# Two alternating sets of semaphores, a projection slab loaded a block earlier, and store waits moved

## The chip, the cores and the metric

The kernel runs on one core of one Trainium2 chip. The metric is the device time of one execution in microseconds; the median of three runs is 5510.2 us (5507.91 to 5512.08).

## What is computed

Two layers of a hybrid trunk, for a prompt of 512 tokens and 8 samples of 8 new tokens (576 rows of 1024, float32). Cut to what matters:

```python
h = _rmsnorm(x, norm_mix[l])
qkv_a, z_a, a_a, b_a, qkv_b, u_c, gate_logits = _split_cols(h @ w_in[l])
o_a, conv_new, delta_new = _deltanet(qkv_a, z_a, a_a, b_a, conv0, delta0, ...)   # gated delta rule, chunks of 128
o_b, wins_new = _dilated_branch(qkv_b, pos0, prompt, wins0)                      # windowed attention, 3 groups of 4 heads
o_c, pool_new = _pool_branch(u_c, pool0, pos0, w_pool[l], pool_scale[l])
gates = sigmoid(gate_logits).reshape(B, T, 3, 1024)
merged = gates[:, :, 0] * (o_a @ wb_a) + gates[:, :, 1] * (o_b @ wb_b) + gates[:, :, 2] * (o_c @ wb_c)
x = x + merged @ w_out[l]
x = x + _peer(_rmsnorm(x, norm_ffn[l]), ...)   # 128 experts per row, fetched by index, up and down
```

The states of the delta rule, the last rows of keys and values of each window group, and the last rows of the two other branches are outputs too.

## The kernel before, in words

TensorE (PE), VectorE (DVE), ScalarE (ACT), GpSimd (POOL) and SyncE (SP) each get a stream of instructions written out by hand, with waits on semaphores. The work of a layer is nine stages, each one `nc.Block()`, and a block ends only when all five engines have arrived: each engine ends with a DRAIN, tells POOL, and POOL releases them all. SP issues most DMAs, POOL issues the gathers, the gate weights and the gate rows, ACT some small ones.

1. `norm_stage` (L287 on): RMS norm of x and its transposed copy hT.
2. `delta_in` (L442): the first 2048 columns of the projection, convolution, norms.
3. `delta_chunks`, first block (L640): per chunk decays and a triangular inverse. POOL starts by copying old cache rows from input to output in HBM.
4. `delta_chunks`, second block (L874): SP loads the delta states of the samples (four loads of 512 KB, L878), PE runs the recurrence over the chunks and then the samples' states; SP stores them (L880, L883) and waits for all five stores.
5. `window_in` (L1288): 2304 columns of the projection in six slabs of 384 columns (1.5 MB each), double buffered. SP issues them through `load_slabs` (L392), the first two at once, later ones when PE has freed the place. PE multiplies (L1321), ACT copies out (L1351), DVE and POOL rotate queries and keys, SP stores key rows (L1280, L1283), PE transposes (L1336), ACT copies (L1358) and then issues twelve stores of value rows. SP waits for the key stores; the value stores are waited for by POOL in the next stage. POOL also loads the first three gate weights.
6. `window_prompt` (L1400): attention of the prompt in 16 units of a row tile and a head. Between the scores PE computes the merge gates (L1220), two halves per unit; ACT copies them out (L1231), POOL stores each finished one to HBM and loads the next weights (L1207, L1202). SP loads the first caches for the next stage.
7. `window_samples` (L1570): attention of the samples over their caches and the rest of the 24 gates. SP loads the pool stage's first slab. POOL waits at the end until all gate stores have landed (L1576).
8. `pool_stage` (L1864): projection to 1536 columns, sliding means, maps. POOL first clears the margins of `ext`; SP loads the first weights and gates for the merge.
9. `score_expert_stage` (L2373): the merge and w_out, the second norm, the routing, then 576 gathers of 128 rows of 8 KB (L2404), a dot product each on DVE (L2429), a diagonal on ACT (L2501) and two products on PE (L2587).

After the last layer `norm_stage` runs once more, and a block stores the result.

Semaphores only count up. There is one set, which all stages share, and a few that are kept (`keep`) and waited for with values that grow by layer. After each stage `clear_semaphores` (L273) adds a block of its own, in which POOL clears the set in two ranges (L282) while the others wait. There are 20 such blocks: nine per layer, one after the initial loads, one in the last norm.

The order in SBUF around the change (in floats per partition): AT_MIX 0 holds hT and branch outputs, AT_LATE 8192 the delta block's zT and cc, later the merge slots, AT_WORK 16384 the work of each stage.

Of the kernel before, what the change touches and what calls it, by code (L numbers as in the profile page):

```python
# [124 lines left out]
class Semaphores:  # L125
# [3 lines left out]
    def __init__(self, make, keep):  # L129
# [4 lines left out]
        self.map1 = make("map1")  # L134
# [6 lines left out]
        self.link_pool = make("link_pool")  # L141
# [16 lines left out]
        self.pool_b = make("pool_b")  # L158
        self.pool_c = make("pool_c")
        self.pool_d = make("pool_d")  # L160
        self.filled = make("filled")
        self.copied = make("copied")
        self.numbers = make("numbers")
        self.paced = make("paced")
        self.dots_done = make("dots_done")
        self.downs_done = make("downs_done")
        self.gelus = make("gelus")
        self.weighted = make("weighted")
        self.diagonal = make("diagonal")
        self.summed = make("summed")  # L170
        self.x_copied = make("x_copied")
        self.gate_in = make("gate_in")
        self.gate_exp = make("gate_exp")
        self.gate_ready = make("gate_ready")
        self.routed = make("routed")
        self.scored = make("scored")
        self.doubled = make("doubled")
        self.values_stored = keep("values_stored")
        self.gcum = make("gcum")
        self.masked = make("masked")  # L180
        self.started = make("started")
        self.inv_sum = make("inv_sum")
        self.inv_done = make("inv_done")
        self.u_sum = make("u_sum")
        self.u_copied = make("u_copied")
        self.x_sum = make("x_sum")
        self.squared = make("squared")
        self.w_out_in = make("w_out_in")
        self.branch_sum = make("branch_sum")
        self.branch_read = make("branch_read")  # L190
        self.gate_open = make("gate_open")
        self.merged_done = make("merged_done")
        self.out_sum = make("out_sum")
        self.x_added = make("x_added")
        self.hT_a = make("hT_a")
        self.hT_b = make("hT_b")
        self.scored0 = make("scored0")
# [5 lines left out]
        self.st_scaled = make("st_scaled")  # L203
        self.ab_read = make("ab_read")
        self.banks_read = make("banks_read")
        self.stored2 = keep("stored2")
        self.pool_slab = keep("pool_slab")
        self.merge_in = [keep(f"merge_in{i}") for i in range(MERGE_RING)]
# [77 lines left out]
def norm_stage(nc, g, gamma, rows, sb, transposed=True, sources=()):  # L286
# [61 lines left out]
    clear_semaphores(nc, g)  # L348
# [64 lines left out]
def delta_stage(nc, g, t, o, l):  # L413
# [12 lines left out]
    clear_semaphores(nc, g)  # L426
    delta_chunks(nc, g, t, o, l, zT, cc, vecs, ab, heads, gb, chunks)
# [5 lines left out]
def delta_in(nc, g, t, o, l, w_in, zT, cc, vecs, ab, heads, ring, slabs, sb):  # L433
# [8 lines left out]
    with nc.Block() as block:  # L442
# [157 lines left out]
SQ = 4 * 512 + H * NS  # L600


def delta_chunks(nc, g, t, o, l, zT, cc, vecs, ab, heads, gb, sb):
# [36 lines left out]
    with nc.Block() as block:  # L640
# [181 lines left out]
        def _(pool):  # L822
            heads2 = lambda ap: ap.rearrange("b t v h d -> b t v (h d)")
# [31 lines left out]
    clear_semaphores(nc, g)  # L855
# [18 lines left out]
    with nc.Block() as block:  # L874
        @block.sync
        def _(sp):
            for h in range(H):
                sp.dma_start(st[:, h], layer(t["state_delta"], l)[:, h].rearrange("b d e -> d b e")).then_inc(s.loaded, 16)  # L878
            sp.wait_ge(s.dve_b, 4)
            sp.dma_start(layer(o["delta_p"], l)[0].rearrange("h d e -> d h e"), state[:, 0]).then_inc(s.stored, 16)  # L880
            for h in range(H):
                sp.wait_ge(s.dve_c, 2 * h + 2)
                sp.dma_start(sd_out[:, h].rearrange("b d e -> d b e"), st[:, h]).then_inc(s.stored, 16)  # L883
            sp.wait_ge(s.stored, 16 * 5)
# [138 lines left out]
        def _(pool):  # L1023
            def spread(half):
# [155 lines left out]
    clear_semaphores(nc, g)  # L1180
# [53 lines left out]
AT_CACHES = AT_WORK + 7296  # L1234
# [3 lines left out]
def window_stage(nc, g, t, o, l, slots):  # L1238
    w_in = layer(t["w_in"], l)
    late, sb = g.space(AT_LATE), g.space(AT_WORK)  # L1240
    qkT = late("qkT", [P, 12, SEQ])
    vals_s, qkT_s = late("vals_s", [P, SW]), late("qkT_s", [P, 12, NS])
    gates = Gates(nc, g, t, l, sb)
    low = sb.above()
    vals = sb("vals", [P, 4, SW])
    window_in(nc, g, t, o, l, w_in, vals, vals_s, qkT, qkT_s, gates, sb.above())
    clear_semaphores(nc, g)
    places = g.space(AT_CACHES)
    caches = Caches(g, t, l, places)
    window_prompt(nc, g, l, vals, qkT, gates, caches, g.space(AT_PROMPT))  # L1250
    clear_semaphores(nc, g)
    window_samples(nc, g, t, l, vals_s, qkT_s, gates, caches, low, places, g.space(AT_LATE + SLOT), slots)
    clear_semaphores(nc, g)
# [6 lines left out]
def window_in(nc, g, t, o, l, w_in, vals, vals_s, qkT, qkT_s, gates, sb):  # L1260

    s = g.s
    ring = sb("ring", [P, 2, KT * WB])
# [5 lines left out]
    heads2 = lambda ap: ap.rearrange("b t v h d -> b t v (h d)")  # L1269
# [3 lines left out]
    def store_rows(eng, kv, done):  # L1273

        count = 0
        for i in range(3):
            src = lambda n: (qk[0:ROWS[n], n, SW + i * 256:SW + (i + 1) * 256], value(n)[:, i * 256:(i + 1) * 256])[kv]
            for n in range(3 if i == 0 else 0, 4):
                at = n * P if i else 0
                eng.dma_start(heads2(layer(o[f"win{i}_p"], l))[0, at:at + P, kv], src(n)).then_inc(done, 16)  # L1280
                count += 16
            keep = min(GROUPS[i][0], PAST + NT)
            eng.dma_start(heads2(layer(o[f"win{i}_s"], l))[:, keep - NT:keep, kv], src(4)).then_inc(done, 16)  # L1283
            count += 16
        assert count == VALUE_STORES
        return count

    with nc.Block() as block:  # L1288
        @block.sync
        def _(sp):  # L1290
            load_slabs(sp, g, ring, [rows_of(w_in)[:, :, C_B + i * WB:C_B + (i + 1) * WB] for i in range(6)])
            sp.wait_ge(s.dve_a, 2 * TILES)
            sp.wait_ge(s.stored, store_rows(sp, 0, s.stored))
# [3 lines left out]

# [46 lines left out]
        def _(act):  # L1344
            for i in range(6):
                for n in range(TILES):
# [32 lines left out]
def window_prompt(nc, g, l, vals, qkT, gates, caches, sb):  # L1379
# [20 lines left out]
    with nc.Block() as block:  # L1400
        @block.sync
        def _(sp):
            caches.ahead(sp)
# [1297 lines left out]
```

## Time and profile before

| | us |
|---|---|
| median of three runs | 5510.2 |
| profiled execution | 5511.6 |
| its span, first to last instruction | 5509.8 |
| PE busy | 4729.3 (86%) |
| DVE busy | 3007.9 (55%) |
| POOL busy | 1542.9 (28%) |
| ACT busy | 1240.7 (23%) |
| DMA over the span | 260 GB/s, 1432.12 MB |

The profile is of one execution. Busy time counts neither waits nor branches nor the issue of DMAs by SP and ACT. The mean granted clock of TensorE is 0.96 of full speed.

### The profile page before, as it was taken

Reading aid. Unit: us, or ns where it says so; the run is one execution under the profiler, and the core shown is the slowest. Engines: PE = TensorE matmul, PEld = TensorE weight load, DVE = VectorE, ACT = ScalarE, POOL = GpSimd, SP = SyncE. Lnnn points to the kernel's source line nnn. Section 1 sums busy time; section 2 is a strip of 40 time slices with the busy share of each in tenths; the row PEclk is TensorE's granted clock in tenths of the full one; section 3 lists DMA queues with packets and bytes.
Section 4 is the critical chain, followed back from the end, with each engine's and each line's share of the span. In section 5 each row is a group of like instructions: output and inputs, shape, how many; then the busy total and the mean of one; then the engine's idle time right before and its main releaser. Section 6 shows DMA issues by size and latency. Waiting matters only on the chain. (4 is left out here: it accounts for less than half of the span.)

```text
span 5509.8 us, 50367 instructions
## 1 busy us (share of the span) xinstructions
PE 4729.3 (86%) x17274; PEld 2768.6 (50%) x17274; DVE 3007.9 (55%) x7296; ACT 1240.7 (23%) x3097; POOL 1542.9 (28%) x1418
## 2 busy tenths in 40 slices
PE   7889999999998777777788899999998987777776
PEld 5765777755444322332167667777554443223321
DVE  4532222226767789975455223231267777999654
ACT  2211220102222233321112112101122222333211
POOL 0321100003444444444304121000044444444442
PEclk9999999999999999999999899999999999999999
DMA  2222232318999999999812232324099999999997
GB/s 100 77 68 85 80 113 79 125 35 342 414 407 411 422 421 421 421 419 421 347 64 77 72 107 66 107 77 143 24 393 416 403 414 421 421 421 421 418 421 303
DMA packets 338777, 1432.12 MB, mean 260 GB/s; under 512 B 27548, under 2 KB 156438, under 8 KB 190602
## 3 DMA queue, kind: packets, MB, share of 16 engines
q0 software_dynamic: 177376, 1268.07, 56.5%
q1 hardware_dynamic: 155214, 157.65, 9.0%
q10 hardware_dynamic: 5932, 3.19, 0.2%
q8 instruction: 137, 2.24, 0.2%
q14 instruction: 118, 0.97, 0.0%
HBM read 1400.18 MB, written 49.44 MB: 263 GB/s over the span
## 5 line engine op out<-in xcount | busy, mean ns | idle before, releaser
L2587 PE MATMUL ps<-early,diag 128*128 128x512 f32 (+1 forms) x3584 | 1693.8, 620 | 390.1 <-ACT diag L2501 389.7
L2404 POOL DMA_INDIRECT early<-in_peer,ids x896 | 979.7, 1093 | 1816.1 <-PE ps L2587 1241.1
L2587 PEld LDWEIGHTS ps<-early,diag 128*128 128x128 f32 (+1 forms) x3584 | 659.4, 191 | 1382.3 <-issue 722.2
L2429 DVE SCALAR_TENSOR_TENSOR early<-early,rows 128x1024 f32<-128x1024 f32 x896 | 1084.5, 1223 | 455.2 <-DMA early<-in_peer,ids 453.8
L2587 PE MATMUL ps<-late,diag 128*128 128x512 f32 (+1 forms) x1024 | 491.0, 626 | 147.3 <-ACT diag L2501 147.1
L2501 ACT ACTIVATE diag<-consts_sb,weight 128x128 f32<-128x128 f32 (+1 forms) x1152 | 392.9, 388 | 702.6 <-DVE weight L2439 697.6
L2587 PEld LDWEIGHTS ps<-late,diag 128*128 128x128 f32 (+1 forms) x1024 | 182.8, 187 | 454.0 <-ACT diag L2501 244.4
L2493 ACT ACTIVATE gel<-dot 128x2 f32<-128x2 f32 x576 | 117.3, 204 | 1292.8 <-DVE early L2429 979.8
L1220 PE MATMUL ps<-hT,gate_ring 128*128 128x288 f32 x1536 | 404.6, 419 | 1.2 <-ACT gate_out L1231 1.2
L2404 POOL DMA_INDIRECT late<-in_peer,ids x256 | 280.3, 1095 | 355.3 <-PE ps L2587 324.0
L2429 DVE SCALAR_TENSOR_TENSOR late<-late,rows 128x1024 f32<-128x1024 f32 x256 | 309.4, 1223 | 121.6 <-DMA late<-in_peer,ids 121.4
L1220 PEld LDWEIGHTS ps<-hT,gate_ring 128*128 128x128 f32 x1536 | 291.6, 194 | 97.8 <-issue 22.2
L1321 PE MATMUL ps<-ring,hT 128*128 128x384 f32 x768 | 255.5, 493 | 26.5 <-DMA ring<-in_w_in 23.3
L2523 PE MATMUL ps<-late 128*128 128x288 f32 x1024 | 259.3, 408 | 5.4 <-ACT late L2174 5.4
L2523 PEld LDWEIGHTS ps<-late 128*128 128x128 f32 x1024 | 195.1, 191 | 78.3 <-issue 23.3
L1492 DVE TENSOR_TENSOR sc<-ps,consts_sb 128x256 f32<-128x256 f32 (+3 forms) x96 | 43.9, 458 | 347.0 <-PE ps L1444 248.4
L1207 POOL DMA_DIRECT2D gate_rows<-gate_out x48 | 27.3, 569 | 698.5 <-ACT gate_out L1231 698.5
L1321 PEld LDWEIGHTS ps<-ring,hT 128*128 128x128 f32 x768 | 146.4, 193 | 131.8 <-DMA ring<-in_w_in 26.4
L362 PE MATMUL ps<-hT,ring 128*128 128x288 f32 x512 | 169.8, 414 | 4.5 <-PEq L278 3.9
L363 PE MATMUL ps<-hT,ring 128*128 128x288 f32 x512 | 167.9, 410 | 0.0
L2439 DVE TENSOR_TENSOR weight<-gel,gates 128x2 f32<-128x2 f32 x576 | 93.1, 162 | 130.7 <-ACT gel L2493 124.7
L1950 PE MATMUL ps<-hT,slot 128*128 128x288 f32 x384 | 127.9, 415 | 11.0 <-PEq L278 11.0
(364 smaller groups left out, 5526.1 us busy)
## 6 DMA issues: line engine op xcount, KB each, us to landing
gate_ring<-in_w_in POOLq DMA_DIRECT2D x48, 512.0 KB, 4.7
ring<-in_w_in SPq DMA_DIRECT2D x12, 1536.0 KB, 6.4
slot<-in_w_branch SPq DMA_DIRECT2D x16, 1152.0 KB, 6.5
ring<-in_w_in SPq DMA_DIRECT2D x8, 2048.0 KB, 9.4
late<-in_peer_query SPq DMA_DIRECT2D x32, 512.0 KB, 17.3
early<-in_peer,ids POOLq DMA_INDIRECT x896, 19.4
gate_rows<-gate_out POOLq DMA_DIRECT2D x48, 288.0 KB, 2.4
slot<-gate_rows SPq DMA_DIRECT2D x16, 864.0 KB, 8.4
```

The costliest lines, as they stand in the source:

```text
L362: nc.tensor.matmul(part_a(g, u), weights(k), rhs(k)[:, 0:HALF], start=k == 0, stop=k == nk - 1)
L363: last = nc.tensor.matmul(part_b(g, u), weights(k), rhs(k)[:, HALF:TOK], start=k == 0, stop=k == nk - 1)
L1220: last = nc.tensor.matmul(g.ps[:, bank, 0:HALF], self.ring[:, i % GATE_RING, k, :], g.hT[:, k, at:at + HALF], start=k == 0, stop=k == KT - 1)
L1321: last = nc.tensor.matmul(g.ps[0:P, u % 4, 0:WB], g.hT[:, k, cols(n)], w[:, k, :], start=k == 0, stop=k == KT - 1)
L1950: nc.tensor.matmul(bank_a(p), weights, g.hT[:, k, 0:HALF], start=k == 0, stop=k == KT - 1)
L2404: pool.indirect_dma_start(place(q), None, table_rows, bass.IndirectOffsetOnAxis(ap=ids[:, n, c:c + 1], axis=0)).then_inc(s.pair[PLACE[q]], 16)
L2429: nc.vector.scalar_tensor_tensor(out=up, in0=up, scalar=1.0, in1=rows[:, n, :], op0=ALU.mult, op1=ALU.mult, accum_out=dot[:, i % 2, k:k + ...
L2439: nc.vector.tensor_tensor(weight[:, i % 2], gel[:, i % 2], gates[:, n, c0:c0 + GROUP], ALU.mult).then_inc(s.weighted, 1)
L2493: nc.scalar.activation(gel[:, i % 2], dot[:, i % 2], ACT.Gelu).then_inc(s.gelus, 1)
L2501: nc.scalar.activation(diag[:, q % DIAGS, 0:ROWS[n]], table(g, "ident" if ROWS[n] == P else "ident2"), ACT.Copy, scale=weight[:, i % 2, k: ...
L2523: last = nc.tensor.matmul(g.ps[:, 4 + i % 2, 0:HALF], late.ring[:, u % Q_RING, k, :], late.hT[:, k, a * HALF:(a + 1) * HALF], start=k == 0 ...
L2587: ins = nc.tensor.matmul(g.ps[0:r, 2 * (n % 2) + m, :], diag[:, q % DIAGS, 0:r], place(q)[:, D + m * 512:D + (m + 1) * 512], start=False, ...
```

## The change

- A stage takes the other of two sets of semaphores than the stage before it (`next_semaphores`), and POOL clears the set that isn't in use at the start of the block. Semaphores that only the expert stage or only the stages of the delta and window branches use are made once and cleared in a stage where nobody uses them. The 20 clearing blocks are gone.
- The first slab of the window projection gets a place of its own (over keys and values of the delta block that are dead by then) and is loaded in the second delta block, behind the states. `window_in` loads slabs 1 to 5.
- SP no longer waits for the stores of the delta states in that block. ACT, DVE and POOL wait for them in `window_in`, ahead of their first write to the places that are stored.
- SP no longer waits for the key stores in `window_in`, but in `window_prompt`, ahead of the cache loads.
- The value stores are issued by SP at the start of `window_prompt`, no longer by ACT at the end of `window_in`.
- POOL no longer waits for the gate stores at the end of `window_samples`; it does at the start of `pool_stage`, before its memsets, and SP does before it loads the first gates. ACT now waits for the memsets before its first copy, DVE before its first.
- Tiles move to make this possible: values to AT_LATE, transposed queries and keys to AT_WORK, scores of the samples in two places, slots in the other order.

```diff
-def clear_semaphores(nc, g):
-    with nc.Block() as block:
-        @block.gpsimd
-        def _(pool):
-            for first, last in g.runs:
-                pool.sem_clear(range(first, last + 1))
+def next_semaphores(g):
+    g.turn = 1 - g.turn
+    g.s = g.sets[g.turn]
+
+def clear_other_set(pool, g):
+    for first, last in g.runs[1 - g.turn]:
+        pool.sem_clear(range(first, last + 1))
+
+def clear_single(pool, runs):
+    for first, last in runs:
+        pool.sem_clear(range(first, last + 1))
...
# norm_stage; every other block with clear_other_set alone at the start of POOL's stream
+            @block.gpsimd
+            def _(pool):
+                clear_other_set(pool, g)
+                clear_single(pool, g.experts_runs)
...
-    clear_semaphores(nc, g)
+    next_semaphores(g)
...
# delta_chunks, second block
             for h in range(H):
                 sp.dma_start(st[:, h], layer(t["state_delta"], l)[:, h].rearrange("b d e -> d b e")).then_inc(s.loaded, 16)
+            sp.dma_start(slab[:], window_slab(t, l, 0)).then_inc(s.win_slab, 16)
             sp.wait_ge(s.dve_b, 4)
-            sp.dma_start(..., state[:, 0]).then_inc(s.stored, 16)
+            sp.dma_start(..., state[:, 0]).then_inc(s.delta_stored, 16)
             for h in range(H):
                 sp.wait_ge(s.dve_c, 2 * h + 2)
-                sp.dma_start(..., st[:, h]).then_inc(s.stored, 16)
-            sp.wait_ge(s.stored, 16 * 5)
+                sp.dma_start(..., st[:, h]).then_inc(s.delta_stored, 16)
...
-AT_CACHES = AT_WORK + 7296
+AT_VALUES, AT_SLAB = AT_LATE + 1536, AT_LATE + 4608
+AT_CACHES = AT_WORK + 10368
...
# window_in
+    ring = (slab, sb("ring", [P, KT, WB]))
...
-            load_slabs(sp, g, ring, [rows_of(w_in)[:, :, C_B + i * WB:C_B + (i + 1) * WB] for i in range(6)])
+            for i in range(1, 6):
+                if i >= 2:
+                    sp.wait_ge(s.slab_free, i - 1)
+                sp.dma_start(ring[i % 2][:], window_slab(t, l, i)).then_inc((s.slab0, s.slab1)[i % 2], 16)
             sp.wait_ge(s.dve_a, 2 * TILES)
-            sp.wait_ge(s.stored, store_rows(sp, 0, s.stored))
+            store_rows(sp, o, l, 0, lambda n, i: qk[...], s.keys_stored)
...
         def _(pool):
+            clear_other_set(pool, g)
+            pool.wait_ge(s.delta_stored, DELTA_STORES * (l + 1))
...
         def _(pe):
-                slab_ready(pe, g, i)
-                w = slab_view(ring, i, KT, WB)
+                w = ring[i % 2]
+                if i == 0:
+                    pe.wait_ge(s.win_slab, 16 * (l + 1))
+                else:
+                    pe.wait_ge((s.slab0, s.slab1)[i % 2], 16 * ((i + 1) // 2))
...
         def _(act):
+                    if i == 5 and n == 0:
+                        act.wait_ge(s.delta_stored, DELTA_STORES * (l + 1))
...
-            act.wait_ge(s.act_b, 6 * TILES)
-            store_rows(act, 1, s.values_stored)
...
         def _(dve):
+            dve.wait_ge(s.delta_stored, DELTA_STORES * (l + 1))
...
# window_prompt
         def _(sp):
+            store_rows(sp, o, l, 1, lambda n, i: (vals[:, n] if n < 4 else vals_s[0:NS])[...], s.values_stored)
+            sp.wait_ge(s.keys_stored, (l + 1) * VALUE_STORES)
             caches.ahead(sp)
...
         def _(pool):
+            clear_other_set(pool, g)
+            clear_single(pool, g.mixing_runs)
...
# window_samples
             for i in range(first_gate // 2, GATE_UNITS):
                 gates.store(pool, i)
-            for i in range(GATE_OUT):
-                pool.wait_ge(s.gate_stored[i], 16 * (l + 1) * (GATE_UNITS // GATE_OUT))
...
# pool_stage
         def _(sp):
             sp.wait_ge(s.slab_free, 2)
+            for i in range(GATE_OUT):
+                sp.wait_ge(s.gate_stored[i], 16 * (l + 1) * (GATE_UNITS // GATE_OUT))
             merge.load(sp, 0)
...
         def _(pool):
+            clear_other_set(pool, g)
+            for i in range(GATE_OUT):
+                pool.wait_ge(s.gate_stored[i], 16 * (l + 1) * (GATE_UNITS // GATE_OUT))
             for i in range(2):
                 nc.gpsimd.memset(ext[:, i, :, 0:PBUF], 0.0).then_inc(s.filled, 1)
...
         def _(act):
+            act.wait_ge(s.filled, 2)
...
         def _(dve):
-                dve.wait_ge(s.filled, 2)
...
+            dve.wait_ge(s.filled, 2)
```

## Rows read from the trace of the kernel before

**Rows 1.** Windows by stage: bounds, length, busy PE, PEld, DVE, ACT, POOL, clock, DMA, GB/s.

```profile
374.56:540.43 165.87, 149.88 (x636) 92.64 (x636) 32.01 (x20) 22.28 (x51) 26.61 (x13) 0.95 0.26 83
...
1021.81:2752.00 1730.19, 1452.10 (x3774) 683.93 (x3774) 1150.61 (x3015) 422.61 (x1140) 619.97 (x576) 0.97 0.89 363
...
3756.90:5486.84 1729.94, 1451.99 (x3774) 683.64 (x3774) 1151.38 (x3015) 422.69 (x1140) 640.05 (x576) 0.97 0.89 363
```

**Rows 2.** Waits of SP's queue over the span: us in total, times, longest.

```profile
SPq L278 <- PEq L278: 13.9, 20, 0.7
...
SPq L874 <- DMA out_delta_s<-st: 5.6, 2, 2.8
```

**Rows 3.** DRAINs of lines 278, 1400 and 1570: ns min/median/max, first and last start.

```profile
L278 POOLq DRAIN  x20: 34/41/47, 17.1 to 5501.4; - x20
...
L1400 POOLq DRAIN  x2: 4948/4980/5012, 744.5 to 3478.5; - x2
...
L1570 SPq DRAIN  x2: 122/122/122, 776.5 to 3511.7; - x2
...
L1570 POOLq DRAIN  x2: 1109/1112/1114, 876.4 to 3610.3; - x2
```

**Rows 4.** Timeline of the pool stage's start, ACT's first copy: start us, us.

```profile
888.98 0.40 ACT L1980 COPY ext<-ps 128x288 f32<-128x288 f32 x1 [15.48 <-PE ps L1951]
```

**Rows 5.** The page's DMA issues: KB each, median us to landing.

```profile
gate_ring<-in_w_in POOLq DMA_DIRECT2D x48, 512.0 KB, 4.7
...
gate_rows<-gate_out POOLq DMA_DIRECT2D x48, 288.0 KB, 2.4
```

**Rows 6.** Timeline from the delta block's end into the window projection, layer 0.

```profile
367.34 3.35 SPq L883 DMA_DIRECT2D out_delta_s<-st  x2
369.01 1.29 DVE L1140 TENSOR_TENSOR st<-st,ps 128x512 f32<-128x512 f32 x2 [1.69 <-PE ps L979]
374.67 1.01 SPq L392 DMA_DIRECT2D ring<-in_w_in  x2
381.12 1.65 PE L1321 MATMUL ps<-ring,hT 128*128 128x384 f32 x2 [11.62 <-DMA ring<-in_w_in]
```

**Rows 7.** Line 392 between 374 and 376 us, the first two slabs' landing.

```profile
DMA to landing us min/median/max: 6.4/8.3/10.1
```

**Rows 8.** Timeline from the window projection's end into the prompt stage, layer 0.

```profile
532.65 0.36 ACTq L1280 DMA_DIRECT2D out_win_p<-vals  x1
532.71 0.65 ACT L1358 COPY qkT_s<-ps 128x256 f32<-128x256 f32 x2
...
538.41 0.61 ACTq L1283 DMA_DIRECT2D out_win_s<-vals_s  x1
...
540.59 0.77 PE L1420 MATMUL ps<-qkT 64*128 64x128 f32 x2 [7.98 <-PEq L278]
```

**Rows 9.** Timeline from the samples' end into the pool stage, layer 0.

```profile
873.79 0.54 POOL L1207 DMA_DIRECT2D gate_rows<-gate_out  x1 [7.20 <-ACT gate_out L1231]
...
878.55 0.82 PE L1950 MATMUL ps<-hT,slot 128*128 128x288 f32 x1 [5.48 <-PEq L278]
```

**Rows 10.** Windows at four stage starts, columns as in rows 1 (last: clock, DMA, GB/s).

```profile
318.80:329.30 10.50, 10.36 (x89) 10.12 (x89) 3.46 (x5) 2.77 (x5) 0.00 (x0) 1.00 0.76 202
...
381.10:385.00 3.90, 3.88 (x6) 2.19 (x7) 0.00 (x0) 0.00 (x0) 0.00 (x0) 0.50 0.97 336
...
540.50:548.90 8.40, 7.28 (x21) 5.65 (x22) 3.65 (x12) 2.70 (x5) 0.00 (x0) 0.50 0.81 243
...
3051.50:3061.10 9.60, 9.48 (x59) 9.51 (x60) 2.13 (x4) 1.79 (x3) 0.00 (x0) 0.68 0.87 223
```

**Rows 11.** Timeline of PE in the prompt stage, the first two times 16 gate products.

```profile
544.82 6.15 PE L1220 MATMUL ps<-hT,gate_ring 128*128 128x288 f32 x16
...
552.08 4.15 PE L1220 MATMUL ps<-hT,gate_ring 128*128 128x288 f32 x16
```

**Rows 12.** Timeline of PE in the second delta block, first products with the loaded states.

```profile
332.26 1.95 PE L936 MATMUL ps<-st,mid 128*32 128x128 f32 x64
```

More of the change, by code:

```diff
@@ L1242, in window_stage @@
     vals_s, qkT_s = late("vals_s", [P, SW]), late("qkT_s", [P, 12, NS])
+    vals = g.space(AT_VALUES)("vals", [P, 4, SW])
     gates = Gates(nc, g, t, l, sb)
[L1244 to L1247, printed above, removed]
+    turned = sb.above()
+    qkT = sb("qkT", [P, 12, SEQ])
+    window_in(nc, g, t, o, l, slab, vals, vals_s, qkT, qkT_s, gates, sb.above())
+    next_semaphores(g)
     places = g.space(AT_CACHES)
@@ L1249, in window_stage @@
     caches = Caches(g, t, l, places)
[L1250 to L1253, printed above, removed]
+    window_prompt(nc, g, o, l, vals, vals_s, qkT, gates, caches, g.space(AT_PROMPT))
+    next_semaphores(g)
+    window_samples(nc, g, t, l, vals_s, qkT_s, gates, caches, turned, g.space(AT_VALUES), places, slots)
+    next_semaphores(g)
@@ L1256, with store_rows @@
 WB = 384
 VALUE_STORES = 16 * 12
-def window_in(nc, g, t, o, l, w_in, vals, vals_s, qkT, qkT_s, gates, sb):
+def store_rows(eng, o, l, kv, rows, done):
+    heads2 = lambda ap: ap.rearrange("b t v h d -> b t v (h d)")
+    count = 0
+    for i in range(3):
+        for n in range(3 if i == 0 else 0, 4):
+            at = n * P if i else 0
+            eng.dma_start(heads2(layer(o[f"win{i}_p"], l))[0, at:at + P, kv], rows(n, i)).then_inc(done, 16)
+            count += 16
+        keep = min(GROUPS[i][0], PAST + NT)
+        eng.dma_start(heads2(layer(o[f"win{i}_s"], l))[:, keep - NT:keep, kv], rows(4, i)).then_inc(done, 16)
+        count += 16
+    assert count == VALUE_STORES
@@ L1376, with window_prompt @@
 LEN_S = (128, 256, 256)
-def window_prompt(nc, g, l, vals, qkT, gates, caches, sb):
+def window_prompt(nc, g, o, l, vals, vals_s, qkT, gates, caches, sb):
     s = g.s
@@ L1553, in ahead, with window_samples @@
         sp.wait_ge(self.g.s.loaded2, 48 * KEY_RING + 80)
-def window_samples(nc, g, t, l, vals_s, qkT_s, gates, caches, low, high, late, slots):
+def window_samples(nc, g, t, l, vals_s, qkT_s, gates, caches, turned, low, high, slots):
     s = g.s
-    sc, stat, apart = low("sc", [P, 2, S_WIDTH]), low("stat", [P, 2, 4]), low("apart", [P, 6, NB, QUAD, NT])
-    kTc = high("kTc", [P, 10 * QUAD, P])
-    pT = late("pT", [P, 2, 8, P])
+    kTc = turned("kTc", [P, 10 * QUAD, P])
+    apart = low("apart", [P, 6, NB, QUAD, NT])
+    pT = high("pT", [P, 2, 8, P])
+    sc, stat = [low("sc", [P, S_WIDTH]), high("sc", [P, S_WIDTH])], low("stat", [P, 2, 4])
     key_rows = (s.slab0, s.slab1, s.map0)
@@ L2600, in build, with common, once, runs_of @@
         numbers = []
-        def keep(name):
-            return ctx.enter_context(nc.semaphore(name))
-        def make(name):
-            sem = keep(name)
-            numbers.append(sem.num)
-            return sem
-        g.s = Semaphores(make, keep)
-        numbers.sort()
-        g.runs, first = [], numbers[0]
-        for a, b in zip(numbers, numbers[1:] + [None]):
-            if b != a + 1:
-                g.runs.append((first, a))
-                first = b
+        def common():
+            made, numbers = {}, []
+            def once(name):
+                if name not in made:
+                    made[name] = ctx.enter_context(nc.semaphore(name))
+                    numbers.append(made[name].num)
+                return made[name]
+            return once, numbers
+        def runs_of(numbers):
+            numbers, runs = sorted(numbers), []
+            first = numbers[0]
+            for a, b in zip(numbers, numbers[1:] + [None]):
+                if b != a + 1:
+                    runs.append((first, a))
+                    first = b
+            return runs
+        (keep, _), (mixing, of_mixing), (experts, of_experts) = common(), common(), common()
+        def one_set(suffix):
+            numbers = []
+            def make(name):
+                sem = ctx.enter_context(nc.semaphore(name + suffix))
+                numbers.append(sem.num)
+                return sem
+            return Semaphores(make, keep, mixing, experts), runs_of(numbers)
+        pairs = [one_set("_0"), one_set("_1")]
+        g.sets, g.runs, g.turn = [made for made, _ in pairs], [runs for _, runs in pairs], 0
+        g.mixing_runs, g.experts_runs = runs_of(of_mixing), runs_of(of_experts)
+        g.s = g.sets[0]
         s = g.s
```

159 lines of the change are left out of this document (77 added, 82 removed).

## Prediction

> **What bounds the kernel now.** I read first the windows by stage. The two stages that fetch and use the experts take 1730.19 and 1729.94 us of the span of 5509.8, at a DMA share of 0.89, and the change touches nothing in them but their borders [rows 1]. They started at unrelated moments and came out 0.25 us apart, so I take them as fixed. The other 2050 us are nine dense TensorE stages per layer (the projection of the window branch has PE busy for 149.88 of 165.87 us). What can be gained there lies at the borders: every stage is a block, and a block ends when its last engine arrives. So the second view is SP's own waits. It shows that SP waited 20 times inside the clearing blocks, 13.9 us in all, and twice, 2.8 us each, for the stores of the delta states to land [rows 2]. Third come the DRAINs, with which each engine arrives at a border: POOL's takes 0.04 us in a clearing block, but 4.98 us where it has just issued a load and 1.11 us even after a wait for its stores [rows 3]. The timelines around three borders per layer give the rest.
>
> **The change, part by part.** The same things happen in both layers, so each is priced once and doubled.
>
> *Clearing blocks.* 20 go: 9 per layer, one at the start, one in the last norm. Each costs SP 0.70 us of waiting [rows 2], and some 0.07 us pass between the border before it and SP's DRAIN; the next stage starts that much later. 20 x 0.77 = 15.4 us. The clears themselves move to POOL at the start of a block, where the profile shows none now. The nearest price is the clearing block itself: the clears cannot cost more than its 0.77 us. They are covered where POOL's first product is wanted late. The tightest place is the pool stage: its memsets are wanted before ScalarE's first copy, which comes 10.5 us into the stage [rows 4], behind PE's first product. POOL there also gets two waits for gate stores that land 2.4 us after their issue [rows 5], that is by 876.2, before the stage starts. ScalarE's and VectorE's waits for the memsets come earlier in their queues than now, but the first thing behind them needs PE's first product anyway. Taken as nothing; the other end, if every clear of the 20 delayed its stage by the 0.4 us of half such a block, is 8 us.
>
> *End of the delta block.* VectorE's last operation ends at 370.30, and SP has issued the last store by 370.69 [rows 6]. It then waits 2.8 us for the landing [rows 2]. That wait goes. SP's own DRAIN does not seem to wait for transfers: in the stage of the samples it took 0.12 us with the pool stage's slab just issued [rows 3]. I take 2.85 us (the wait and the check behind it), 5.7 for two. The low end is 0, if that DRAIN held for stores as POOL's does. The new waits of ScalarE, VectorE and POOL for these stores stand in a stage where SP's wait shows them landed before it even starts.
>
> *The slab loaded ahead.* SP issues the first slab of the window projection at 374.67; it lands 6.4 us later and PE starts at 381.12 [rows 6, 7]. With the slab there PE starts at once: 6.4 us, 12.9 for two. What is late next is slab 1, now issued first in the stage. The pair issued together had both landed 10.1 us after the first issue [rows 7], and PE works over 20 us on one slab (149.88 us for six), so it is hidden. Its issue loses its partner, so it lands no later. SP's queue in the delta block: the slab's issue stands behind the four loads of states and before two kinds of stores whose inputs come 30 us later, so it can delay only the states.
>
> *End of the window projection.* ScalarE's last copy is over at 533.36; its twelve issues of value stores run from 532.65 to 539.02, and its DRAIN and the border follow at once. PE starts at 540.59 [rows 8], so the border fell at about 539.7, a clearing block and 0.1 us earlier. Without the issues it falls some 0.15 us after the last copy, at 533.5 to 533.6: 6.1 us, 12.2 for two. SP takes over the twelve issues, about 6.4 us, in the next stage, ahead of the wait for the key stores (issued 30 us earlier) and of the loads of caches. These are wanted one stage later, some 200 us off, so 6.4 us on SP are covered. Key stores: SP's wait is only removed; SP had been done long before ScalarE, so this alone gives nothing.
>
> *End of the samples.* POOL issues the last gate store at 873.79 to 874.33 and it lands at 876.2 [rows 5, 9]. POOL's wait for it ends then, its DRAIN takes another 1.11 us, and PE starts at 878.55. The wait goes to the pool stage, but the DRAIN stays, and where POOL had a transfer in flight its DRAIN lasted 4.98 us [rows 3], with a load of some 4.7 us to landing issued in front of it [rows 5]. So I expect the DRAIN to hold the border until the landing and a little (0.4 us) over, 876.6 in place of 877.5: 0.9 us, 1.8 for two. The ends are 0 (landing and then the whole 1.11) and 3.1 (no holding at all).
>
> [...]
>
> *The clock.* After an idle stretch PE is granted half the clock, 1.2 GHz. At the start of the window projection this held for 3.9 us, at the start of the prompt stage, after 7.98 us of idle PE, for 8.4 us [rows 8, 10]. In that stretch 16 products of the gates took 6.15 us, later 16 of them take 4.15 [rows 11], so 2.0 us, and with the slow scores in front about 2.7, are lost. After the change PE is idle there for little over 1 us. The nearest rows are the starts of the second delta block, after 1.8 us of idle: full clock in layer 0, a mean of 0.68 in layer 1 [rows 10]. So half of it, 1.3 us, 2.6 for two; ends 0 and 5.4. At the start of the projection PE comes from sparse work at half clock with or without the change: nothing, with 1.5 us per layer either way in the range.
>
> *Rearranged tiles* (values, keys, scores, slots) run the same instructions in the same order: nothing.
>
> Sum: 15.4 + 5.7 + 12.9 + 12.2 + 1.8 + 2.6 = 50.6 us. The profiled execution took 5511.6 us (span 5509.8 and 1.8 around it), which gives 5461.0. It was 1.4 us above the median of the three runs, 5510.2; against the median 5459.6. I say 5460.
>
> **The rivals.**
>
> *Less: borders are held by something else.* SP's DRAIN holds for the state stores (5.7 lost) and POOL's for its full length after landing (1.8 lost). For it: POOL's DRAINs. Against: SP's 0.12 us. 50.6 - 7.5 = 43.1, so 5467. The same size has a second form: the 1.5 MB slab shares the engines with the 2 MB of states. These are moved in the first 10.5 us of the block at 202 GB/s [rows 10], and PE wants them at 332.26, about 3 us later [rows 12]. If both were served evenly the states would end 7 us later, PE would stall 4 us, 8 in both layers: 5468. Against it: of two slabs issued 0.4 us apart the first landed 3.7 us before the other [rows 6, 7], so an earlier issue is mostly served first.
>
> *More: the DRAIN of POOL does not wait and the clock stays up.* 4.4 + 2.8 more, 57.8 us: 5452. [...]
>
> *Slower.* The expert stages lose more than the borders give. The two hold 1152 gathers, one every 3.0 us (3460 us by 1152), and they start some tens of us earlier, at another place of the clock's rhythm. From 44 ns more on each gather (1.5%) the 50.6 us are gone, from 54 ns it is slower by 0.2%; at 60 ns, 69 us, the time is 5529. Against it: the two stages of this trace, started at unrelated times, differ by 0.25 us, not by 30 [rows 1].
>
> *The change doesn't do what it says.* The slab lies in the tiles of the delta block and could be held until that block is over, or the clears could still be waited for at each border: then the 12.9 or the 15.4 us stay, 5473 to 5475. The code has PE wait for the slab alone, and nobody for the clears, so little speaks for it.
>
> **The numbers.** The forecast gets 0.72, the two forms of less 0.13, more 0.09, not doing what it says 0.03, slower 0.01, and a drift of the expert stages that just eats the gain 0.02. The range of 5450 to 5471 holds the first three with their bounds (clears 8 us at one end, clock 5.4 at the other). A measurement of this kernel tells 0.2%, 11 us, from no change; every case but the last two is beyond it on the fast side: faster 0.97, same 0.02, slower 0.01.
>
> **What would show it.** No blocks that only clear, and POOL's clears at the start of blocks with nobody waiting for them. PE's first product of the window projection within 0.2 us of the border, the border within 0.5 us of SP's last issue of state stores. ScalarE with no issue after its last copy of the projection, SP with twelve stores at the start of the prompt stage. A DRAIN of POOL of about 2.2 us at the end of the samples. Expert stages of 1730 us. Wrong would be: PE waiting for states at the first product with them, a DRAIN of SP of microseconds, an expert stage off by more than 5 us.

## The result, and the profile after

The changed kernel takes 5463.2 us in the median of four runs (5460.2 to 5466.3), the kernel before, on the same chip, 5511.1 (5507.9 to 5513.5). The ratio is 0.9914, 95% interval 0.9896 to 0.9931: 48 us less, where 50 were forecast (5460), and inside the range. The profiled execution took 5460.2 us, 51.4 us less in its span than before.

From the pages, span and PE's share of before and of after (before had PE 4729.3, 86%):

```profile
span 5458.4 us, 50113 instructions
PE 4732.1 (87%) x17274; PEld 2768.4 (51%) x17274; DVE 3010.3 (55%) x7296; ACT 1241.3 (23%) x3097; POOL 1556.0 (29%) x1418
```

PE is as busy as before, in a shorter span. The stages, from one release to the next (in before the clearing block that stood behind a stage counts with it); "priced" is what the prediction's terms come to, stage by stage, for both layers:

| both layers | before | after | less | priced |
|---|---|---|---|---|
| load, norms, store | 76.1 | 71.4 | 4.7 | 3.1 |
| delta projection | 327.7 | 323.0 | 4.8 | 1.5 |
| delta, first block | 237.4 | 237.0 | 0.4 | 1.5 |
| delta, second block | 112.8 | 101.1 | 11.7 | 7.2 |
| window projection | 331.7 | 305.0 | 26.7 | 26.6 |
| prompt | 420.0 | 417.9 | 2.1 | 4.1 |
| samples | 255.9 | 259.4 | -3.5 | 3.3 |
| pool | 288.0 | 286.2 | 1.8 | 1.5 |
| experts | 3460.1 | 3457.4 | 2.7 | 1.5 |

The total is right; the samples are 6.8 us off, and the delta projection and the second delta block by 3.3 and 4.5 us. The windows of the second delta block and the samples, in before (columns as in rows 1; layer 0, then layer 1):

```profile
318.78:373.79 55.01, 45.39 (x382) 35.54 (x382) 25.26 (x48) 14.29 (x49) 14.68 (x6) 0.85 0.29 82
750.43:877.62 127.19, 120.59 (x820) 99.34 (x820) 24.71 (x53) 18.38 (x38) 8.94 (x13) 0.88 0.32 103
...
3051.46:3107.74 56.28, 46.52 (x382) 36.80 (x382) 25.25 (x48) 14.30 (x49) 14.69 (x6) 0.83 0.29 81
3484.37:3611.56 127.19, 120.56 (x820) 99.10 (x820) 24.72 (x53) 18.38 (x38) 8.94 (x13) 0.88 0.32 103
```

And the same view of after, with the window projection, the prompt stage, the pool stage and the two expert stages (which answer to [rows 1]):

```profile
312.90:363.47 50.57, 43.53 (x382) 33.91 (x382) 25.26 (x48) 14.30 (x49) 14.69 (x6) 0.91 0.37 110
363.47:515.95 152.48, 149.84 (x636) 92.64 (x636) 31.94 (x20) 22.32 (x51) 26.62 (x13) 0.99 0.23 75
515.95:724.77 208.82, 199.93 (x932) 147.43 (x932) 57.19 (x128) 45.89 (x97) 23.32 (x32) 0.98 0.29 92
724.77:856.17 131.40, 125.22 (x820) 102.77 (x820) 24.71 (x53) 18.38 (x38) 8.95 (x13) 0.84 0.31 100
856.17:999.25 143.08, 136.49 (x552) 105.28 (x552) 49.56 (x106) 18.53 (x40) 4.97 (x10) 0.97 0.32 101
999.25:2726.77 1727.52, 1456.38 (x3774) 686.10 (x3774) 1150.94 (x3015) 423.06 (x1140) 641.41 (x576) 0.97 0.89 364
3023.01:3073.58 50.57, 43.46 (x382) 33.91 (x382) 25.26 (x48) 14.30 (x49) 14.69 (x6) 0.91 0.37 110
3435.20:3563.23 128.03, 122.03 (x820) 99.28 (x820) 24.71 (x53) 18.39 (x38) 8.95 (x13) 0.86 0.32 102
3706.36:5436.24 1729.88, 1450.87 (x3774) 683.84 (x3774) 1152.67 (x3015) 422.83 (x1140) 631.44 (x576) 0.97 0.89 363
```

Read the count and the clock together. The samples run the same 820 products; PE is busy 125.22 us at a mean clock of 0.84, 122.03 at 0.86, 120.59 at 0.88. Only two levels are granted, full and half, so a mean of 0.84 is half the clock for twice 0.16 of the stage: about 42 us in layer 0 (2 x 0.16 x 131.4), 36 in layer 1, 31 before. The stage took longer because TensorE had half the clock for longer. The second delta block went the other way: 0.85 and 0.83 before, 0.91 now.

The border into the window projection, the timeline of after (answers to [rows 6]):

```profile
359.83 3.35 SPq L904 DMA_DIRECT2D out_delta_s<-st  x2
...
361.49 1.29 DVE L1162 TENSOR_TENSOR st<-st,ps 128x512 f32<-128x512 f32 x2 [1.69 <-PE ps L999]
363.58 0.38 SPq L1320 DMA_DIRECT2D ring<-in_w_in  x1
...
363.63 4.75 PE L1354 MATMUL ps<-slab,hT 128*128 128x384 f32 x8 [1.64 <-PEq L894]
```

PE begins 0.16 us after the border at 363.47, which itself falls 0.29 us after SP's last issue. The border into the prompt stage (answers to [rows 8]), and PE behind it:

```profile
514.88 0.92 ACT L1393 COPY qkT_s<-ps 128x256 f32<-128x256 f32 x3
516.06 0.33 SPq L1294 DMA_DIRECT2D out_win_p<-vals  x1
...
516.11 0.90 PE L1458 MATMUL ps<-qkT 64*128 64x128 f32 x6 [1.07 <-PEq L1314]
```

```profile
519.62 6.57 PE L1242 MATMUL ps<-hT,gate_ring 128*128 128x288 f32 x16
...
527.31 4.15 PE L1242 MATMUL ps<-hT,gate_ring 128*128 128x288 f32 x16
```

ScalarE issues nothing any more and SP does. But PE, idle for only 1.07 us, still has half the clock for its first 16 gate products, 6.57 us against 4.15. It doesn't bring the half clock along: the windows around this border show full clock until 1.75 us into the stage, and then half for 6.8 us.

```profile
505.00:515.95 10.95, 10.04 (x72) 7.05 (x70) 0.00 (x0) 4.21 (x11) 0.00 (x0) 1.00 0.00 0
515.95:517.70 1.75, 0.90 (x6) 0.74 (x6) 0.58 (x2) 1.28 (x1) 0.00 (x0) 1.00 0.23 77
517.70:524.50 6.80, 6.45 (x16) 4.88 (x17) 3.07 (x10) 1.41 (x4) 0.00 (x0) 0.50 0.62 194
```

The DRAINs at the ends of the second delta block, of the prompt stage and of the samples, and the clears (answers to [rows 3]):

```profile
L894 SPq DRAIN  x2: 123/124/124, 363.2 to 3073.4; - x2
```

```profile
L1434 POOLq DRAIN  x2: 4898/5032/5166, 719.7 to 3429.9; - x2
```

```profile
L1609 SPq DRAIN  x2: 122/122/122, 752.6 to 3462.9; - x2
...
L1609 POOLq DRAIN  x2: 2955/2958/2960, 853.1 to 3560.2; - x2
```

```profile
L286 POOLq EVENT_SEMAPHORE_RANGE_CLEAR  x19: 219/219/225, 16.0 to 5436.3; - x19
```

SP's lasts 0.12 us with stores in flight, POOL's 2.96 us behind the last gate store. The states are there when PE wants them: its first product with them starts at 326.37, 13.4 us into the block, as before (332.26, 13.5 us). The range clears (19 of 0.22 us, 5 shorter ones on other lines) have nobody waiting for them.

### The profile page after: what moved, and what is told of

Its sections match the earlier page's. It is cut to its first block and busy times, and to the rows that moved or that the text cites. A ratio compares the mean times of both kernels' runs of the same rounds, so it can differ in the third digit from the quotient of the medians.

```text
span 5458.4 us, 50113 instructions
## 1 busy us (share of the span) xinstructions
PE 4732.1 (87%) x17274; PEld 2768.4 (51%) x17274; DVE 3010.3 (55%) x7296; ACT 1241.3 (23%) x3097; POOL 1556.0 (29%) x1418
## 5 line engine op out<-in xcount | busy, mean ns | idle before, releaser
L2449 POOL DMA_INDIRECT early<-in_peer,ids x896 | 993.0, 1108 | 1807.2 <-PE ps L2632 1239.8
L1993 PE MATMUL ps<-hT,slot 128*128 128x288 f32 x384 | 128.1, 416 | 7.9 <-PEq L1609 7.9
L1354 PE MATMUL ps<-slab,hT 128*128 128x384 f32 x384 | 129.2, 498 | 4.5 <-PEq L894 3.3
L1354 PE MATMUL ps<-ring,hT 128*128 128x384 f32 x384 | 126.3, 487 | 1.9 <-PE ps L1358 1.9
## 6 DMA issues: line engine op xcount, KB each, us to landing
gate_rows<-gate_out POOLq DMA_DIRECT2D x48, 288.0 KB, 2.4
```

What stands on the lines that cost most here:

```text
L1354: last = nc.tensor.matmul(g.ps[0:P, u % 4, 0:WB], g.hT[:, k, cols(n)], w[:, k, :], start=k == 0, stop=k == KT - 1)
L1993: nc.tensor.matmul(bank_a(p), weights, g.hT[:, k, 0:HALF], start=k == 0, stop=k == KT - 1)
L2449: pool.indirect_dma_start(place(q), None, table_rows, bass.IndirectOffsetOnAxis(ap=ids[:, n, c:c + 1], axis=0)).then_inc(s.pair[PLACE[q]], 16)
```

## The experiments

Each kernel is compared with runs of before on its own chip. Executions of one kernel spread over some 10 us, so single microseconds are read from stages, not from medians.

**The changed kernel again** (e0_changed_again).

> The changed kernel itself, once more, beside which the others of this call are read. Theory (borders): 0.991 of before, 5463 us, and the same borders as in its first profile. The samples' stage of layer 0 was 3.4 us longer in that profile than before the change, where I had forecast 1.7 less. If that is the clock's rhythm (theory), its length moves by some us from profile to profile with the time at half clock, and the delta block and both layers differ too; if it is the moved tiles or the queues (rival), layer 0's samples stage is again near 131.4 us and layer 1's near 128.0.

Measured: 5465.1 us against 5508.9 before, ratio 0.9918 (0.9904 to 0.9932). 43.8 us this time. The samples, layers 0 and 1:

```profile
727.23:858.62 131.39, 125.25 (x820) 102.42 (x820) 24.71 (x53) 18.36 (x38) 8.93 (x13) 0.84 0.31 100
3440.71:3572.12 131.41, 125.23 (x820) 102.85 (x820) 24.71 (x53) 18.35 (x38) 8.93 (x13) 0.84 0.31 100
```

Layer 0 is again at 131.4 us, as the rival has it; layer 1, which had 128.0, now has 131.4 too. So the same code gives both lengths in layer 1, and this run alone doesn't decide between the two theories.

**Clearing blocks put back** (e1_clearing_blocks).

```diff
-def next_semaphores(g):
+def next_semaphores(g, nc):
     g.turn = 1 - g.turn
     g.s = g.sets[g.turn]
+    with nc.Block() as block:
+        @block.gpsimd
+        def _(pool):
+            clear_other_set(pool, g)
+            clear_other_set(pool, g)
```

> The changed kernel with a block after each stage again in which POOL clears twice and the others wait. Borders theory: 20 x 0.77 = 15.4 us more than the changed kernel, and each such block 0.7 to 0.8 us on every engine. Rival (the blocks were covered, and the gain of the change lies elsewhere): less than 5 us more.

Measured: 5477.7 us, ratio 0.9943 (0.993 to 0.9957), 12.6 us above the changed kernel, 2.8 less than expected. SP's wait in these blocks:

```profile
SPq L280 <- PEq L280: 13.3, 20, 1.0
```

The blocks are nearly as long as they were (0.74 to 0.76 us but one of 1.04, 15.2 in all between the borders; 15.3 in before). What is missing came back elsewhere: the samples took 126.4 and 124.6 us net of their block, against 131.4 and 128.0.

**Slab late** (e2_slab_late).

```diff
 # delta_chunks, second block
-            sp.dma_start(slab[:], window_slab(t, l, 0)).then_inc(s.win_slab, 16)
 # window_in
+            sp.dma_start(slab[:], window_slab(t, l, 0)).then_inc(s.win_slab, 16)
             for i in range(1, 6):
```

> The changed kernel with slab 0 issued at the start of the window projection, in front of slab 1. Borders theory: PE starts 6.4 us after the border, 12.9 us more in all. Rival (the early slab costs the delta block something): less than 10 us more, because the delta block gets shorter by what the slab cost it.

Measured: 5476.3 us, ratio 0.9939 (0.9926 to 0.9953), 11.2 above. The projection took 159.5 us in both layers in place of 152.5, 14.0 more, of which 1.1 wasn't expected: the slab took 7.4 us from its issue to PE's start, not 6.4. PE's start, in the timeline of this kernel, whose border is at 365.18:

```profile
365.30 0.38 SPq L1316 DMA_DIRECT2D slab<-in_w_in  x1
...
372.67 1.01 PE L1354 MATMUL ps<-slab,hT 128*128 128x384 f32 x1 [8.97 <-DMA slab<-in_w_in]
```

The second delta block lasted 50.58 and 50.57 us with and without the slab in it: the slab doesn't delay the states.

**Value stores on ScalarE** (e3_act_stores).

```diff
 # window_in, ScalarE
+            act.wait_ge(s.act_b, 6 * TILES)
+            store_rows(act, o, l, 1, lambda n, i: value(n)[:, i * 256:(i + 1) * 256], s.values_stored)
 # window_prompt, SyncE
-            store_rows(sp, o, l, 1, ..., s.values_stored)
```

> The changed kernel with the twelve value stores issued by ScalarE at the end of the window projection again. Theory: that border falls 6.1 us later, 12.2 us more for two, and 1 to 3 us more from PE's longer idle time and the half clock behind it at the start of the prompt stage. Rival (the stores only change place): less than 6 us.

Measured: 5478.0 us, ratio 0.9944 (0.9931 to 0.9958), 12.9 above. The projection took 158.6 us in both layers, 6.1 more. The timeline of this kernel, from ScalarE's last copies to PE's start:

```profile
514.76 0.65 ACT L1393 COPY qkT_s<-ps 128x256 f32<-128x256 f32 x2
...
520.46 0.61 ACTq L1297 DMA_DIRECT2D out_win_s<-vals_s  x1
...
521.88 1.61 PE L1459 MATMUL ps<-qkT 64*128 64x128 f32 x6 [7.22 <-PEq L1314]
```

The prompt stage behind it, after 7.2 us of idle PE, took 209.5 and 209.7 us against 208.8 and 209.1: this long idle time costs 0.6 to 0.7 us of clock per layer more than 1.07 us does, half of the 1.3 in the sum.

**The wait for the state stores back** (e4_state_wait).

```diff
                 sp.dma_start(..., st[:, h]).then_inc(s.delta_stored, 16)
+            sp.wait_ge(s.delta_stored, DELTA_STORES * (l + 1))
```

> The changed kernel with SP waiting for the stores of the delta states at the end of the second delta block again. Theory: that border 2.8 us later, 5.7 us more in all. Rival (SP's DRAIN holds for stores anyway): nothing more.

Measured: 5471.4 us, ratio 0.993 (0.9917 to 0.9944), before at 5510.9. The block took 53.39 and 53.38 us in place of 50.57, and SP's wait is there again:

```profile
SPq L894 <- DMA out_delta_s<-st: 5.6, 2, 2.8
```

**POOL's wait for the gate stores back** (e5_gate_wait).

```diff
                 gates.store(pool, i)
+            for i in range(GATE_OUT):
+                pool.wait_ge(s.gate_stored[i], 16 * (l + 1) * (GATE_UNITS // GATE_OUT))
```

> The changed kernel with POOL waiting for the gate stores at the end of the samples again. Theory (POOL's DRAIN holds the border until the store has landed and a little more): the DRAIN takes 1.1 us in place of 2.96, the border falls 0.8 to 1 us later, 1.8 us more in all, hardly to be measured. Rival (a DRAIN of POOL costs the same always): 3.1 us per layer, 6 in all.

Measured: 5466.5 us, ratio 0.9918 (0.9905 to 0.9932). The samples took 132.15 us in place of 131.40 in layer 0, 0.75 more, and 128.67 in place of 128.03. DRAIN in this kernel:

```profile
L1609 POOLq DRAIN  x2: 1106/1108/1111, 856.3 to 3573.6; - x2
```

It starts after the wait and lasts 1.11 us; without the wait it starts at once, lasts 2.96, and the border comes some 0.75 us earlier. The rival's 3.1 us per layer are out.

**Gate stores deferred** (e6_samples_store; e7_deferred_gates). POOL issues the last gate store of the samples first in the pool stage; in e7 it also issues the prompt stage's last store and load first in the samples.

```diff
 # e6
-            for i in range(first_gate // 2, GATE_UNITS):
+            for i in range(first_gate // 2, GATE_UNITS - 1):
                 gates.store(pool, i)
 # pool_stage, POOL, ahead of its waits for the stores
+            merge.gates.store(pool, GATE_UNITS - 1)
 # e7, besides: window_prompt, then window_samples
-            for i in range(len(units)):
+            for i in range(len(units) - 1):
-            for i in range(first_gate // 2, GATE_UNITS - 1):
+            for i in range(first_gate // 2 - 1, GATE_UNITS - 1):
```

> The changed kernel with POOL's last gate store (and load) of the prompt stage and of the samples each issued as the first thing of the next stage, so that no transfer of POOL is in flight at these borders. Theory (POOL's DRAIN waits for transfers in flight): both DRAINs fall below 0.2 us, the prompt stage's border falls at VectorE's last copy, 3.5 us earlier, the samples' at ScalarE's, 2.4 to 2.6 us earlier, 12 us less in all than the changed kernel. Rival (the DRAINs have a fixed length of 5 and 3 us): nothing less. The next gate's weights arrive 6 us later, which PE should not notice, since it wants them three units on.

> The changed kernel with one thing more: POOL issues the last gate store not at the end of the samples, but first in the pool stage. This is half of the run that deferred both and came out about 20 us below the changed kernel, where 12 were expected. POOL's DRAIN then ends before ScalarE's last copy, so the border falls about 3.3 us earlier (856.17 against 852.42 + 0.40 + 0.1), 6.6 us for both layers. If an earlier border also keeps TensorE at full clock at the start of the pool stage (it had half clock for 6 us there), another 2 to 3 us per layer come on top: about 11 us below the changed kernel's, 5454. If only the wait counts: 6.6 us, 5458.

Measured: e7 5444.1 us, ratio 0.9876 (0.9861 to 0.9891), some 20 us below the changed kernel where 12 were expected. Its DRAINs did not fall below 0.2 us, as expected; POOL's still last 3 to 7 us, behind the store (and load) before, but start so early that they are over ahead of the border:

```profile
L1435 POOLq DRAIN  x2: 5064/5848/6631, 709.4 to 3412.7; - x2
...
L1610 POOLq DRAIN  x2: 3045/3048/3050, 843.2 to 3543.5; - x2
```

The borders are at 722.77 and 850.88. e6 5451.3 us, ratio 0.9891 (0.9874 to 0.9907), about 13 below. The stages of the samples and of the pool in e6, each in both layers:

```profile
725.43:853.65 128.22, 125.25 (x820) 102.27 (x820) 24.71 (x53) 18.38 (x38) 8.41 (x12) 0.84 0.31 100
853.65:993.77 140.12, 133.20 (x552) 103.20 (x552) 49.55 (x106) 18.52 (x40) 5.51 (x11) 0.98 0.34 105
3432.54:3557.30 124.76, 122.03 (x820) 99.43 (x820) 24.71 (x53) 18.39 (x38) 8.42 (x12) 0.86 0.31 103
3557.30:3697.27 139.97, 131.77 (x552) 102.26 (x552) 49.47 (x106) 18.52 (x40) 5.52 (x11) 1.00 0.33 105
```

The samples are 3.2 us shorter each at an unchanged clock: POOL's DRAIN. The pool stage is some 3.1 shorter each (143.1 in after), though nothing was taken from it. The first 7 us of the pool stage, in after and then in e6:

```profile
856.17:863.17 7.00, 6.84 (x16) 5.00 (x17) 0.00 (x0) 0.00 (x0) 0.20 (x2) 0.55 0.80 205
```

```profile
853.65:860.65 7.00, 6.84 (x28) 5.43 (x29) 0.00 (x0) 0.00 (x0) 0.54 (x1) 1.00 0.84 211
```

16 products in the same time as 28. PE's idle time at this border, 3.94 us in after, is 0.74 in e6 and in e7, whose line is:

```profile
851.04 0.72 PE L1995 MATMUL ps<-hT,slot 128*128 128x288 f32 x2 [0.74 <-PEq L1610]
```

With it the clock stays up: in both layers of e6, e7 and e8 PE has full clock in the stage's first 7 us, and in both layers of all other traces, with 3.9 us idle or more, it has half the clock for at least 3.4 us. In e7 the prompt stage took 205.3 us in place of 208.8 and 209.1, the samples 128.1 and 125.1 in place of 131.4 and 128.0, the pool stage 140.5 and 140.1: 7.3, 6.2 and 5.6 us less.

**Everything deferred** (e8_deferred_all): e7, and SP doesn't wait for the pool rows' stores; VectorE and ScalarE do, in the expert stage.

```diff
 # pool_stage (its stores now count on a kept semaphore)
-            sp.wait_ge(s.stored, 16 * (2 + NB))
 # expert stage, behind the merge, on VectorE and on ScalarE
+            dve.wait_ge(s.rows_stored, 16 * (2 + NB) * (l + 1))
+            act.wait_ge(s.rows_stored, 16 * (2 + NB) * (l + 1))
```

> As the one with deferred gates, and SP doesn't wait for the stores of the pool branch's rows at the end of the pool stage; VectorE and ScalarE wait for them in the expert stage behind the merge. Theory: the pool stage's border falls at ScalarE's last scaling, 2.7 us earlier, 5.4 us less than with deferred gates, 17 us less than the changed kernel, about 5446 us. Rival (the expert stage, bound by its gathers, ends when it ends): its gathers start as much earlier, so no rival time short of the clock's few us.

Measured: 5436.9 us (5434.8 to 5437.7), ratio 0.9864 (0.9849 to 0.9879): 74 us below before. It beats both kernels. The pool stage is some 3 us shorter than in e7, 137.25 and 137.07 us, and the expert stages behind it, 1727.8 and 1727.9 us, don't give that back. It is 9 us faster than expected, most of it e7's 8.

**A shifted start** (f1_one_empty, f2_two_empty, f4_four_empty). Does the samples' clock go by when the stage starts, or by the change's work in it?

```diff
 # window_samples, ahead of its block; K = 1, 2, 4
+    for _ in range(K):
+        with nc.Block() as block:
+            @block.gpsimd
+            def _(pool):
+                clear_other_set(pool, g)
```

> One empty block (a clear by POOL, two borders' worth of handshake, 0.77 us) is put in front of the stage of the samples in each layer. Question: do the 131.39 and 128.03 us that this stage took in the two layers of the changed kernel (half clock for 41.5 and 35.0 us), against 127.96 and 127.96 before (31.8 and 31.6), come from when the stage starts, or from the change's own work in it? If from the start, then a small shift alone moves the stage's half-clock time by some us in either direction and its length with it, between the values that all runs so far show (125.1, 128.0, 131.4 us); the total moves by 1.5 us plus or minus 6. If from the change's work, both layers keep 131.4 and 128.0 us and the total is 1.5 us above the changed kernel's.

> Two empty blocks in front of the stage of the samples in each layer, 1.5 us of shift per layer. If the stage's length goes by when it starts: 125.1, 128.0 or 131.4 us behind the border, not in step with the shift, total 3.1 us more plus or minus 6. If by its work: 131.4 and 128.0 us again, total 3.1 us above the changed kernel's.

> Four empty blocks in front of the stage of the samples in each layer, 3.1 us of shift per layer. If the stage's length goes by when it starts: 125.1, 128.0 or 131.4 us, total 6.2 us more plus or minus 6. If by its work: 131.4 and 128.0 us again, total 6.2 us above the changed kernel's.

Measured: 5464.2, 5457.0 and 5461.4 us, ratios 0.9916 (0.9899 to 0.9932), 0.9904 (0.9888 to 0.9921) and 0.9905 (0.9889 to 0.9922). Such a block isn't quite empty: POOL clears one range in it, where the clearing blocks of before have two. It costs 0.5 us, not 0.77 (one of the fourteen took 0.76). The samples behind it, layers 0 and 1, in f1, then in f2:

```profile
726.20:853.97 127.77, 122.08 (x820) 99.95 (x820) 24.72 (x53) 18.38 (x38) 8.96 (x13) 0.86 0.31 102
3443.90:3570.30 126.40, 120.63 (x820) 99.50 (x820) 24.72 (x53) 18.38 (x38) 8.96 (x13) 0.88 0.32 104
```

```profile
725.45:851.86 126.41, 120.58 (x820) 99.10 (x820) 24.71 (x53) 18.35 (x38) 8.93 (x13) 0.88 0.31 104
3432.12:3558.59 126.47, 120.64 (x820) 98.99 (x820) 24.78 (x53) 18.35 (x38) 8.93 (x13) 0.88 0.32 104
```

The same code, 1.0 us later, in 126.4 and 126.5 us in place of 131.4 and 128.0; half a microsecond of shift gave 127.8 in one layer and 126.4 in the other. Before the change it was 127.2 less the 0.77 us of the border, 126.4 too. The lengths differ by clock alone, and the work of the change in the stage did not cause them. So the second theory is out for the stage. Two points of the expectation failed: I took 125.1, 128.0 and 131.4 for the only values, and f2 comes out below its bound (3.1 - 6), since the pool stage behind it shortened too, to 141.8 and 141.6 us. As totals the three runs can't be told from the changed kernel, so added blocks are no improvement shown. Whether a start is lucky by its place in time or by the idle time in front of it, these runs leave open, since the added blocks move both (PE's idle time in front of the stage was 4.8 and 5.6 us in f1, 5.2 in f2, 4.2 and 4.4 in after). That layer 1 took 128.0 us in after and 131.4 in e0, with 4.4 and 4.2 us idle, speaks for the place.

## Why the prediction came out

(A layer has eight dense stages beside the experts, not nine as the prediction counts; no term hangs on it.)

*Clearing blocks, 15.4 us.* The size was right: 15.2 us of blocks between the borders when they are put back. The clears cost nothing where they are now, as assumed.

*End of the delta block, 5.7.* Right: 2 x 2.8 in the run that puts the wait back. SP's DRAIN of 0.12 us rules out the rival in which it holds for stores. One reading was wrong without harm: the stores have not landed before the next stage starts, now that nobody waits for them, but some 3 us into it; the first operations of VectorE and POOL there wait for ScalarE for about 80 us anyway. The other 4.5 us that the two blocks gained in the trace (11.7 against 7.2) were in no term. They are clock, 0.91 against 0.85 and 0.83, and not a steady gain: in e5, f1 and f4 one of the two blocks took 53.8 us (a mean of 0.85 in f4), with the change in it.

*Slab and value stores, 12.9 and 12.2.* Right: the stage lost 26.7 us of 26.6 priced. Put back singly they cost 14.0 and 12.2 us in the stage.

*End of the samples, 1.8.* Right in size and in cause: the border holds until the last gate store has landed. From the store's issue to the border it took 3.83 us before (873.79 to 877.62) and 3.06 after (853.11 to 856.17): 0.77 per layer for 0.9. The expected DRAIN of 2.2 us was counted from the end of the issue, its record begins with the issue: 2.96. That POOL's DRAIN waits for a transfer, e6 shows: it took the transfer from in front of it and got 3.2 us per layer. The Trainium skill ("VectorE: DVE Perf Modes", "The DRAIN you can't avoid") gives about 12 ns, constant, for the DRAINs of the runtime's preamble and postamble. No trace here shows those, and the figure is no price for a DRAIN at a block's end.

*The clock, 2.6.* This is the term that was mis-sized. I took half of the loss at the prompt stage's start to go with the idle time. Over both layers the stage gave 0.6 us beyond its two clearing blocks, and with the stores put back it cost 1.3. The step that failed is that the half clock there comes from the idle time: after 1.07 us of idle it falls 1.75 us into the stage and stays low for 6.8 us, over the same gate products as after 7.98. Why it falls there isn't shown; in that stretch PE was busy for 0.90 of 1.75 us. The rows I leaned on, the starts of the second delta block, are another border. At the pool stage it does work: 3.94 us of idle, half clock; 0.74 in e6 and e7, full clock.

*What was in no term.* The samples gave back 6.8 us (-3.5 for 3.3) by half clock, which I had treated as fixed everywhere but at one border. The gains of clock in the delta stages (4.5 and 3.3), 1.6 in the load and the norms and 1.2 in the experts covered it, so that 50.6 priced met 51.4 in the spans. That close agreement is luck: the shift runs move the samples alone by up to 5.4 us per layer. The medians, 47.9 and 43.8 us of gain in two measurements, show how far it can be trusted.

*Rivals.* The expert stages came out at 1727.5 and 1729.9 us, over all runs 1726.4 to 1731.0: no drift with the start, the slower rival is out. "More" needed a DRAIN that doesn't wait: out for POOL. "Less" needed a DRAIN of SP that holds, or states that come late: both out (0.12 us, and no stall at the first product with them). The change does what it says: the slab's 12.9 and the blocks' 15.4 us are gone.

## What to carry to other kernels

A block border costs what its latest engine does last. List, for each border, every engine's arrival and DRAIN: here a store issued by GpSimd just ahead of it held everybody until it had landed (3 us, and 3 more of clock behind the samples), a store issued by SyncE held nobody. Move such issues past the border first; that was worth some 20 us on top of the change, and some 27 with SyncE's wait for the pool rows moved too. And read each stage's length together with its mean clock before you give a difference of a few microseconds to an edit.

## What the runs showed of the hardware

- POOL's DRAIN lasts until its own transfers have landed, and some 0.5 us more (2.96 us for a store that lands in 2.4, 4.90 and 5.17 with a load behind it), SP's does not (0.12 us with state stores under way).
- Idle time of TensorE at a border can have a second price: at the pool stage, after 3.94 us, 16 products in the first 7 us in place of 28 after 0.74. It isn't idle time alone: at the prompt stage the clock fell after 1.07 us of it as well, 1.75 us into the stage.
- The stage of the samples, not edited itself, took between 124.6 us (e1) and 131.4 us, at mean clocks of 0.88 to 0.84. An added microsecond can shorten what follows: 126.4 us in f2.
- A block in which POOL only clears costs 0.5 us with one range clear in it (13 of 14) and 0.74 to 0.78 with two (39 of 40).
